# The second layer's modulation on VectorE instead of TensorE, in a kernel of two blocks

## What is computed

```python
c_act, cc_act = silu(c), silu(c_ctx)            # two vectors of 2048
for i in range(2):                              # layer 0 retention, layer 1 attention
    mod_l = c_act @ ada_w[i] + ada_b[i]         # ada_w[i] is 2048 x 6144
    mod_c = cc_act @ ada_w[i] + ada_b[i]
    sh, sc, gt = split(mod, 3)                  # shift, scale, gate, for each of the two
    h = rms_norm(x, gain[i]) * (1 + sc) + sh
    x = x + gt * mixer(h)
x = second_block(x)
```

## Time and profile before

| | |
|---|---|
| median of 3 runs | 3269.02 us |
| profiled execution, span from first to last instruction | 3265.3 us |
| TensorE busy, matmuls | 3195.3 us, 98% |
| VectorE busy | 1757.6 us, 54% |
| ScalarE busy | 1298.9 us, 40% |
| mean granted clock of TensorE | 0.995 |
| chain that ended last | TensorE 90%, VectorE 4%, ScalarE 2%, DMA 2% |
| loads of the stream | 936 chunks of 512 KB, median 4.2 us to landing |

### The profile page before, as it was taken

One profiled execution on the slowest core, in us unless ns is written; L12 is line 12 of the kernel. 1 busy time (PEld: TensorE's weight loads), 2 busy tenths in 40 slices (PEclk: granted clock), 3 DMA queues, 4 the chain that ended last, 5 costly groups with the idle time before them and its releaser, 6 DMA issues.

```text
span 3265.3 us, 48483 instructions
## 1 busy us (share of the span) xinstructions
PE 3195.3 (98%) x20556; PEld 2772.3 (85%) x20556; DVE 1757.6 (54%) x2600; ACT 1298.9 (40%) x1878; POOL 0.2 (0%) x4
## 2 busy tenths in 40 slices
PE   8999999999999999999998999999999999999998
PEld 6677777878778787777876889988999999999998
DVE  5543544444444444444446667778676665555555
ACT  4443222232322323222234645556554444444443
POOL 0000000000000000000000000000000000000000
PEclk9999999999999999999999999999999999999999
DMA  9854433233333333323334434445655545556564
GB/s 369 317 192 174 174 110 133 93 110 136 116 123 104 116 110 128 130 104 119 107 123 162 133 106 146 152 130 172 199 167 180 172 154 168 181 189 199 194 194 149
DMA packets 153928, 508.98 MB, mean 156 GB/s; under 512 B 15345, under 2 KB 35953, under 8 KB 152945
## 3 DMA queue, kind: packets, MB, share of 16 engines
q1 hardware_dynamic: 149328, 493.03, 44.4%
q10 hardware_dynamic: 4384, 12.85, 1.0%
HBM read 501.62 MB, written 4.19 MB: 155 GB/s over the span
## 4 chain that ended last, share of the span: by engine, by line
PE 90%; DVE 4%; ACT 2%; DMA 2%; issue 1%; SPq 1%; ACTq 0%; DVEq 0%
PE bank L590 28%; PE bank L592 27%; PE bank L591 27%; PE bank L652 3%; PE bank L835 1%; DMA raw<-stream 1%; DVE w_lo L1677 1%; PE bank L816 1%; ACT w_hi L1084 1%; PE bank L826 1%; SPq L563 0%; PE bank L668 0%; ACT a_s L1392 0%; DVE a_s L2084 0%; DMA raw_h<-stream 0%
## 5 line engine op out<-in xcount | busy, mean ns | idle before, releaser
L590 PE MATMUL bank<-h_hi,w_hi 128*128 128x256 f32 (+1 forms) x4032 | 1259.7, 312 | 10.7 <-DVE w_lo L1677 5.1
L592 PE MATMUL bank<-h_hi,w_lo 128*128 128x256 f32 (+1 forms) x4032 | 1239.8, 307 | 0.0
L591 PE MATMUL bank<-h_lo,w_hi 128*128 128x256 f32 (+1 forms) x4032 | 1239.1, 307 | 0.0
L1677 DVE TENSOR_TENSOR w_lo<-raw,w_hi 128x1024 fp32r<-128x1024 f32 x729 | 881.5, 1222 | 585.7 <-ACT w_hi L1084 581.3
L1084 ACT ACTIVATE w_hi<-raw 128x1024 fp32r<-128x1024 f32 x729 | 761.5, 1057 | 914.3 <-PE bank L592 568.7
L590 PEld LDWEIGHTS bank<-h_hi,w_hi 128*128 128x128 f32 x4032 | 759.3, 188 | 83.4 <-issue 39.2
L591 PEld LDWEIGHTS bank<-h_lo,w_hi 128*128 128x128 f32 x4032 | 759.6, 188 | 44.9 <-issue 3.1
L592 PEld LDWEIGHTS bank<-h_hi,w_lo 128*128 128x128 f32 x4032 | 759.1, 188 | 43.8
L590 PE MATMUL bank<-w_hi,h_hi 128*128 128x512 f32 x704 | 286.6, 407 | 12.5 <-DVE w_lo L1677 6.2
L592 PE MATMUL bank<-w_hi,h_lo 128*128 128x512 f32 x704 | 276.6, 393 | 0.0
L591 PE MATMUL bank<-w_lo,h_hi 128*128 128x512 f32 x704 | 275.9, 392 | 0.0
(11 more groups left out here) (257 smaller groups left out, 2890.4 us busy)
## 6 DMA issues: line engine op xcount, KB each, us to landing
raw<-stream SPq DMA_DIRECT2D x904, 512.0 KB, 4.2
raw_h<-stream SPq DMA_DIRECT2D x32, 512.0 KB, 10.0
res<-tokens_in ACTq DMA_DIRECT2D x4, 1024.0 KB, 8.8
vg<-mem_in ACTq DMA_DIRECT2D x4, 512.0 KB, 8.7
h_hi<-mem_kv ACTq DMA_DIRECT2D x2, 1024.0 KB, 9.7
out<-res SPq DMA_DIRECT2D x4, 512.0 KB, 3.0
mem_kv<-qk ACTq DMA_DIRECT2D x1, 1024.0 KB, 7.9
mem_kv<-vg ACTq DMA_DIRECT2D x1, 1024.0 KB, 7.5
```

The lines of the kernel that those rows point to most:

```text
L590: pe.matmul(out, sh, mh, start=start, stop=False, **checks)
L591: pe.matmul(out, sh, ml, start=False, stop=False, **checks)
L592: return pe.matmul(out, sl, mh, start=False, stop=stop, **checks)
L1677: dve.tensor_tensor(in_quarters(m.low(raw)[:, :]), m.raw[SLOT[raw]], in_quarters(m.w_hi[slot][:, :]).bitcast(F32), ALU.subtract).then_inc( ...
```

## The change

The 96 chunks of layer 1 are laid out by output feature instead of by input feature: partition p holds, for two feature tiles k = 2t and 2t+1, the weights of feature p of the tile from 512 of the 2048 inputs (a quarter q). There are 4 quarters of 24 pairs, so still 96 chunks. VectorE multiplies such a chunk with the conditioning vector, which lies as a row on every partition (`c_rows`, 128 x 1024, 512 KB, one for each quarter), and sums along the free axis, starting from the sum of the quarter before or from the bias. That is four instructions of 512 elements for a chunk. The vector is written to DRAM once at the start, and broadcast to all partitions four times from SyncE's queue. The product with the gain follows once, in the last head. TensorE's modulation matmuls and turns for layer 1, ScalarE's copies and VectorE's additions are gone.

The chunks lie behind other places: in heads 1 to 6 behind q/k tiles 0 to 3, g tiles 0 and 2, value chunks 4 to 7, and ret_out chunks 0, 2, 4, 6 and 7 (15 in a head), and in head 7 behind tiles 0 to 5. The queue of loads now waits for the last of a chunk's four instructions on VectorE ahead of loading into its slot.

```diff
-for _h in range(1, RET_HEADS - 1):
-    BESIDE[_h] = modulation_beside(places_of_head((1,) * 8, (1,) * 8), [(1, n) for n in range(3 * _h - 3, 3 * _h)])
-
-BESIDE[RET_HEADS - 1] = modulation_beside(
-    places_of_head((1,) * 6 + (0,), ()) + [(("o",), 2), (("t", 7), 0)] + [(("r", n), 2) for n in range(KT // 2)],
-    [(1, n) for n in range(18, 24)])
+for _h in range(1, RET_HEADS):
+    BESIDE[_h] = {}
+
+MOD_QUARTERS, MOD_PAIRS = 4, MOD_TILES // 2
+MOD_K = P // MOD_QUARTERS
+
+
+def modulation_on_vector():
+
+    steps = [(q, t) for q in range(MOD_QUARTERS) for t in range(MOD_PAIRS)]
+    out = {}
+    for h in range(1, RET_HEADS):
+        places = [("t", i) for i in ((0, 1, 2, 3, 4, 6) if h < RET_HEADS - 1 else range(6))]
+        if h < RET_HEADS - 1:
+            places += [("v", c) for c in range(4, 8)] + [("r", n) for n in range(0, 8, 2)] + [("r", 7)]
+        for place in places:
+            if steps:
+                out[(h, *place)] = steps.pop(0)
...
 NEEDS = []
 for _c in range(CHUNKS):
-    _n = BEFORE[_c] + 1 if BEFORE[_c] is not None and RAW_USE[BEFORE[_c]] else 0
+    _n = BEFORE[_c] + 1 if BEFORE[_c] is not None and (RAW_USE[BEFORE[_c]] or MOD_USE[BEFORE[_c]]) else 0
     NEEDS.append(max(_n, NEEDS[-1] if NEEDS else 0))
...
+RELOAD = {WHERE["ada", 0, MOD_TILES // 2 - 1][3] + 12: 0}
+for _q in range(1, MOD_QUARTERS):
+    RELOAD[FIRST["mod", _q - 1, MOD_PAIRS - 1] + SLOTS] = _q
...
         slot, before = SLOT[c], BEFORE[c]
-        if before is not None and RAW_USE[before]:
-            sp.wait_ge(s.mm, before + 1)
+        if before is not None and MOD_USE[before]:
+            sp.wait_ge(*s["modded"].at(*STREAM[before][0][1:]))
+        elif before is not None and RAW_USE[before]:
+            sp.wait_ge(s.mm, DONE[before])
         elif before is not None:
             sp.wait_ge(s.lo, Q[before] + 1)
         sp.dma_start(m.raw[slot], in_quarters(d["stream"][c])).then_inc(s.raw[slot], 16)
+        if c in RELOAD:
+            q = RELOAD[c]
+            if q == 0:
+                sp.wait_ge(s.load["c_out"], 16)
+                sp.wait_ge(*s["ada_turned"].at(*GROUPS[-1]))
+            else:
+                sp.wait_ge(*s["modded"].at(q - 1, MOD_PAIRS - 1))
+            rows = d["c_rows"][MOD_K * q:MOD_K * (q + 1), :].rearrange("a b -> (a b)").unsqueeze(0)
+            sp.dma_start(m.c_rows[:, :, :, :].rearrange("p a b c -> p (a b c)"), rows.broadcast_to([P, MOD_K * 2 * KT])
+                         ).then_inc(s.load["c_rows"], 16)
...
+            if half and n == 3:
+                act.wait_ge(*s["cond_rows"].at())
+                act.dma_start(d["c_rows"], flat(m.cond_rows)).then_inc(s.load["c_out"], 16)
...
+    def modulate(q, t):
+
+        c = FIRST["mod", q, t]
+        dve.wait_ge(s.raw[SLOT[c]], 16 * USE[c])
+        if t == 0:
+            dve.wait_ge(s.load["c_rows"], 16 * (q + 1))
+        if q:
+            dve.wait_ge(*s["modded"].at(q - 1, t))
+        for j in range(2):
+            k = 2 * t + j
+            w = m.raw[SLOT[c]][:, 2 * j:2 * j + 2, :].rearrange("p a (b c) -> p (a b) c", c=KT)
+            for b in range(2):
+                x = m.mod[1][:, k, b:b + 1]
+                start = x if q else m.bias1[:, 1, k - KT:k - KT + 1] if KT <= k < 2 * KT else m.param("ada_b1", k, 1)
+                i = dve.tensor_tensor_reduce(out=w if b else m.products[:, j, :, :], in0=w, in1=m.c_rows[:, :, b, :], scale=1.0, scalar=start,
+                                             op0=ALU.mult, op1=ALU.add, accum_out=x)
+        i.then_inc(*s["modded"].up(q, t))
+
+    def modulated():
+
+        dve.wait_ge(*s["modded"].at(MOD_QUARTERS - 1, MOD_PAIRS - 1))
+        dve.tensor_tensor(m.mod[1][:, KT:2 * KT, :], m.mod[1][:, KT:2 * KT, :],
+                          m.param("gain1").unsqueeze(2).broadcast_to([P, KT, 2]), ALU.mult).then_inc(*s["mod1_set"].up())
+
     def beside(h, *place):
         for layer, n in BESIDE[h].get(place, ((), (), ()))[2]:
             ada_add(layer, n)
+        if (h, *place) in MODS:
+            modulate(*MODS[(h, *place)])
...
             if last and n < 7:
                 for j in range(2):
                     add_square("x1", 2 * n + j, BOTH)
-                beside(h, "r", n)
+            beside(h, "r", n)
+            if last and n == 0:
+                modulated()
...
+    for c, (what, name, layer, k0, nk, n0, nn) in enumerate(STREAM):
+        if what[0] == "mod":
+            block = w[name][layer][:, n0:n0 + 2 * P].reshape(KT, P, 2, P)[:, k0:k0 + MOD_K]
+            stream[c].reshape(P, 2, MOD_K, KT)[...] = block.transpose(3, 2, 1, 0)
+            continue
```

More of the change, by code:

```diff
@@ L126 @@
 BESIDE[0] = modulation_beside(places_of_head((2, 2, 3, 2, 3, 2, 3, 3), (2, 2, 2, 2, 2, 2, 0, 0)), [(0, n) for n in range(16, 24)])
-for _h in range(1, RET_HEADS - 1):
-    BESIDE[_h] = modulation_beside(places_of_head((1,) * 8, (1,) * 8), [(1, n) for n in range(3 * _h - 3, 3 * _h)])
-BESIDE[RET_HEADS - 1] = modulation_beside(
-    places_of_head((1,) * 6 + (0,), ()) + [(("o",), 2), (("t", 7), 0)] + [(("r", n), 2) for n in range(KT // 2)],
-    [(1, n) for n in range(18, 24)])
+for _h in range(1, RET_HEADS):
[12 more added lines that the diff above has]
+                out[(h, *place)] = steps.pop(0)
+    assert not steps, len(steps)
+    return out
+MODS = modulation_on_vector()
 AV_AK = [("av", n) for n in range(5)] + [("ak", 0), ("ak", 1), ("av", 5), ("ak", 2), ("av", 6), ("ak", 3), ("av", 7)]
@@ L161, in beside @@
             ada(layer, n, (c,))
+        if (h, *slot) in MODS:
+            q, t = MODS[(h, *slot)]
+            out.append((("mod", q, t), "ada_w", 1, MOD_K * q, 0, 2 * P * t, 0))
     beside("start", "begin")
@@ L257 @@
 RAW_USE = [b[0][0] == "ada" for b in STREAM]
-SPLIT = [c for c in range(CHUNKS) if not RAW_USE[c]]
+MOD_USE = [b[0][0] == "mod" for b in STREAM]
+SPLIT = [c for c in range(CHUNKS) if not RAW_USE[c] and not MOD_USE[c]]
 Q = [0]
-for _raw in RAW_USE:
-    Q.append(Q[-1] + (not _raw))
+for _c in range(CHUNKS):
+    Q.append(Q[-1] + (not RAW_USE[_c] and not MOD_USE[_c]))
+DONE = [_c + 1 - sum(MOD_USE[:_c + 1]) for _c in range(CHUNKS)]
 WIDEST = WHERE["mv", 1][7] // (2 * WIDE) * (2 * WIDE)
@@ L358 @@
     "n_meaned", "n_rstd", "n_scaled", "merged", "m_hi", "m_lo", "final")
-LOADS = ("par", "tab", "tok0", "tok1", "tok2", "tok3", "mem_in0", "mem_in1", "mem_in2", "mem_in3", "rope0", "attn_tables", "block_tables", "kv_out", "kv_in", "out")
+LOADS = ("par", "tab", "tok0", "tok1", "tok2", "tok3", "mem_in0", "mem_in1", "mem_in2", "mem_in3", "rope0", "attn_tables", "block_tables", "kv_out", "kv_in", "c_out", "c_rows", "out")
 class Signals:
@@ L422, in __init__ @@
         modulated = nc.sbuf_base
+        self.c_rows = nc.alloc_sbuf_tensor_at("c_rows", [P, MOD_K, 2, KT], F32, offset=modulated)
         self.cond = sb("cond", [P, KT, 32])
@@ L860, in tensor_program @@
         mm.then_inc(s.mm, 1)
-        if c == 1:
-            beside(RET_HEADS - 1, "end")
     for h in range(GROUP):
@@ L1090, in done @@
     def done(what, n=2):
-        act.wait_ge(s.mm, WHERE[what][n - 1] + 1)
+        act.wait_ge(s.mm, DONE[WHERE[what][n - 1]])
     def psum(*what):
@@ L1683, in done @@
     def done(what, n=2):
-        dve.wait_ge(s.mm, WHERE[what][n - 1] + 1)
+        dve.wait_ge(s.mm, DONE[WHERE[what][n - 1]])
     def psum(*what):
@@ L1968, in vector_program @@
             weights_to(WHERE["ret_out", h][n], 1 if last and n == 7 else SLOTS)
-            dve.wait_ge(s.mm, WHERE["ret_out", h][n] + 1)
+            dve.wait_ge(s.mm, DONE[WHERE["ret_out", h][n]])
             if h == 0:
@@ L2353 @@
     stream = np.empty((CHUNKS, P, CHUNK), np.float32)
-    for c, (_, name, layer, k0, nk, n0, nn) in enumerate(STREAM):
+    for c, (what, name, layer, k0, nk, n0, nn) in enumerate(STREAM):
[3 more added lines that the diff above has]
+            continue
         block = w[name][layer][k0 * P:(k0 + nk) * P, n0:n0 + nn]
@@ L2384, in program @@
         d["out"] = nc.dram_tensor("out", (P, KT, L), F32, kind="ExternalOutput").ap()
+        d["c_rows"] = nc.dram_tensor("cond_rows", (P, 2 * KT), F32, kind="Internal").ap()
         d["mem_kv"] = nc.dram_tensor("mem_kv", (P, KT, L), F32, kind="Internal").ap()
```

22 lines of the change are left out of this document (12 added, 10 removed).

## The result

The changed kernel takes 3380.64 us (median of four runs, 3377.05 to 3385.81) against 3269.44 for the kernel before in the same session: ratio 1.0342, 95% interval 1.0328 to 1.0355, so 3.4% slower. The forecast was 3395 with a range of 3345 to 3475.

A forecast was written before the change was run, and what follows sets the result against it. TensorE was taken to bound heads 1 to 7, with VectorE's round becoming the period after the change. Terms -82 + 196.2 + 8.3 + 3.9 = +126 on 3265.3 gave 3391.7, so 3395 as median; range 3345 to 3475.

The forecast's parts named there:

- The step M: VectorE's four multiply-and-sum instructions on one modulation chunk: 4 x 0.75 = 3.0 us, bounds 2.7 to 3.7.
- The half-rate rival: Two float32 SBUF sources run VectorE's step at half rate, M 5.3 us: 3584 us, chance 8%.
- the 2% case with M at 1.4: VectorE's step takes half the cycles, so the time stays the same: 3265 us, chance 2%.
- the 3% case in which the release is hidden everywhere: Late freeing of raw slots costs nothing and all 82 us of TensorE's relief are won: 3187 us, chance 3%.
- The reload: From raw slot free through DMA and w_hi to both w_lo: 7.16 us, with a scatter of 0.2 us.
- The round: VectorE's loop in a q/k tile: 2.81 + M + 7.16 + 0.1 = 13.07 us, where TensorE takes 11.68 today.
- The head: One of heads 1 to 6: 198.3 us less TensorE's relief plus 32.7 us idle gives 220.4 us.
- The load of c_rows: Reloading the conditioning row on SyncE's queue: 1.3 us each, three times in the chain, 3.9 us.
- the rival in which only the q/k rounds bind: Loads beside v and ret_out come earlier than counted, so only q/k tiles lose time: 3257 us, chance 6%.
- 200 us of idle time: Sign to look for: TensorE idle, released by w_lo, in pieces of 2 to 5 us, some 200 in all.
- the clock costs next to nothing inside the chain: Slower TensorE costs nothing inside the chain; only at g tile 1 up to 1.7 us per head, 0 to 12.
- The theory of the release: Raw slots freed only after VectorE's step, behind eviction, swap and rotation, make VectorE's round the period in heads 1 to 7.

The follow-up runs named there:

- spread2: Changed kernel with each step ahead of VectorE's wait for TensorE and places spread more evenly, some moved to head 0 and the last head: 3182.54 us.
- warm: Changed kernel with 8 to 16 extra unread matmuls on TensorE in nine waits of heads 1 to 6 and five of head 7: 3384.91 us.
- before_late: Kernel before, extra unneeded VectorE work (2.65 us) at each place of heads 1 to 6, and slot loads waiting for that work: 3319.73 us.
- before_extra: Kernel before, with the same extra unneeded VectorE work at each place of heads 1 to 6, but no added wait: 3269.51 us.
- dup_ahead: Changed kernel with two extra 1024-element products on VectorE ahead of each of the 96 steps, before the slot is freed: 3596.5 us.
- dup_behind: Changed kernel with the same two extra products behind each of the 96 steps, after the slot is freed: 3417.38 us.
- late_spread: Changed kernel with its order kept (step behind eviction and additions) but places spread over eight tiles, value chunks and ret_out: 3285.38 us.
- spread: Changed kernel with places spread and each step ahead of VectorE's wait for TensorE: 3200.41 us.

## Why the prediction was right, step by step

**The step M.** Assumed 3.0 us, measured 2.77 (1088.83 to 1091.60): four instructions 0.67 apart and the last one's 0.75. The lower bound of 2.7 was near; the forecast was 0.23 too long. The rows by shape, 500 to 1785:

```profile
L1765 DVE CUSTOM_DVE_ANT_1 raw<-raw,c_rows,mod 128x512 f32<-128x512 f32 x138 | 103.5, 750 | 0.0
L1765 DVE CUSTOM_DVE_ANT_1 products<-raw,c_rows,mod 128x512 bf16<-128x512 f32 x138 | 103.2, 747 | 0.0
L1765 DVE DVE_READ_ACCUMULATOR2_ANT mod<- 128x1 f32 x352 | 29.9, 85 | 0.0
```

L1917, the row that I took it from, has 743 ns. The sum's read-out takes 85 ns, and the next instruction starts at the same moment (1089.50), so it costs nothing. The Trainium skill (VectorE: DVE Perf Modes, Two Vector instructions with no wait between them) says that an operation which also writes its accumulator is two instructions; the rows agree, with 85 ns for the second.

**The half-rate rival** (8%, 3584 us) falls with the same rows: 512 elements from two float32 sources take 750 ns, not 1.22 us. By the rule of the Trainium skill (Vector Engine (DVE) Microarchitecture Reference, Points that are easy to get wrong) they would have; for this operation the measurement decides against it. The page names the form S2S2D2_STT, and the trace shows this operation as CUSTOM_DVE_ANT_1; no run says whether the rule was meant for it. With M at 2.77 the 2% case with M at 1.4 falls too, and with rounds of 12.3 to 12.9 the 3% case in which the release is hidden everywhere.

**The reload.** Assumed 7.16 from the slot's release to the end of both w_lo, measured 6.8 to 7.4, 7.39 in the round shown (1091.60 to 1098.99), mean 7.0 without the round that holds a load of c_rows. To the start of the first w_hi it is 3.1 to 3.8, where the forecast had 3.5.

**The round.** Forecast 10.07 + M = 13.07. Of the 21 q/k rounds of heads 1 to 7, 20 are 12.3 to 12.9, mean 12.5. With 2.81 to the step, M 2.77 and a reload of 7.0 that is 12.6, less 0.1 by which the eviction starts ahead of w_lo's end. Of the 0.57 that I was over, 0.23 is M, some 0.16 the reload, 0.1 the semaphore, for which I had no row and which the reload as measured holds already, and the rest the overlap of eviction and w_lo.

**The relief of TensorE.** 12 chunks at 0.80 and 3 turns at 0.35 taken from 198.3 gives 187.7 for a head; `spread2` has 187.64.

**The head.** Forecast 220.4; the six are 217.8 to 222.2, mean 219.4. That the two lie so close is in part luck, since two errors of opposite sign meet in a head. From the step behind v chunk 4 to that behind the next head's last q/k tile the forecast had 145.6 us (2.4 to 148.0), and the six stretches took 139.8 to 143.1, mean 141.0, with the loads of c_rows in them: the rounds are shorter. Against that the first step comes later than forecast in every head: 5.73 us behind TensorE's start on v chunk 3 and not 2.4, so 3.3 late. The forecast left out what VectorE does there: it normalizes the head's outputs behind v chunk 2 (L2002, L2005, 980.09 to 984.99 in head 3), and only then come the w_lo of v6 and the step.

```profile
980.30 0.39 PE L631 MATMUL bank<-w_hi,h_hi 128*128 128x512 f32 x1
...
983.10 1.89 DVE L2005 TENSOR_TENSOR o_lo<-vg,o_hi 128x512 fp32r<-128x512 f32 x3
984.90 1.22 DVE L1718 TENSOR_TENSOR w_lo<-raw,w_hi 128x1024 fp32r<-128x1024 f32 x1
986.04 0.75 DVE L1765 CUSTOM_DVE_ANT_1 products<-raw,c_rows,mod 128x512 bf16<-128x512 f32 x1
```

The sum for all heads can be followed by the first tiles. First tile to first tile, head 1 to head 7, and the last head's four tiles (line L1943 and, of the kernel before, L1874; durations in ns, first and last start):

```profile
L1943 DVE TENSOR_SCALAR qk<-bank x25: 682/684/692, 431.8 to 1748.3; 128x512 f32<-128x512 f32 x25
...
L1943 DVE TENSOR_SCALAR qk<-bank x4: 683/684/685, 1748.3 to 1785.7; 128x512 f32<-128x512 f32 x4
```

```profile
L1874 DVE TENSOR_SCALAR qk<-bank x4: 691/692/692, 1623.8 to 1658.8; 128x512 f32<-128x512 f32 x4
```

The six heads take 1316.5 us and took 1190.0 (6 x 198.3): +126.5. The last head's tiles take 37.4, not 35.0: +2.4. Behind them 1590.0 us remain of 3375.7 where it was 1606.5 of 3265.3: -16.5, which fits the chunks that TensorE no longer multiplies there. Head 1's first tile comes 2.0 earlier. Together +110.4, the difference of the two spans. The forecast had +126; by its own steps the six heads were 6 x 22.1 and 3.9, so 136.5, which is 10 more than measured. What is left of it, -10, was measured as -16. So the forecast lies 16 us above the difference of the spans.

**The load of c_rows** was under-counted: 1.3 us each. In the round of head 4 that holds one, the two w_hi stand 3.26 us apart (1120.83 and 1124.09) instead of 1.27, and the round is 14.91 instead of 12.5. So 2.0 to 2.4. Three of them are 2 to 3 us more than forecast in all.

**Where the wait shows.** The places were right: TensorE's gaps in the changed kernel divide about evenly between the tiles and ret_out, which speaks against the rival in which only the q/k rounds bind (6%, 3257 us). TensorE's groups by shape, 500 to 1785, with the idle time ahead of each in the last column: the tiles, then ret_out.

```profile
L631 PE MATMUL bank<-h_hi,w_hi 128*128 128x512 f32 x732 | 295.8, 404 | 65.6 <-DVE w_lo L1718 65.6
...
L631 PE MATMUL bank<-o_hi,w_hi 128*128 128x512 f32 x384 | 163.8, 427 | 61.4 <-DVE w_lo L1718 61.3
```

The amount was not: 200 us of idle time were forecast and 127 are there. In head 4 TensorE needs 187.6 and has 222.16: 34.5 us to lose, near the forecast of 32.7. It is idle only 21.4 of them; the other 13 are a slower TensorE (clock 0.94). That the clock costs next to nothing inside the chain was argued in the forecast and fits `warm`. Behind the chain it costs what the forecast allowed: from g tile 1 to v chunk 3, where TensorE binds, four of the six heads take 62.6 us at full clock and two take 64.2, with the clock at 0.83 over the first 10 us; the forecast had up to 1.7 for each. The time lost was forecast rightly; as a sign to look for, "some 200 us of waiting" was wrong, since idle time and slow matmuls share one gap.

**The theory of the release** is shown by `before_late` against `before_extra` (the same work, one wait more, 50 us) and, in the changed kernel itself, by `dup_ahead` against `dup_behind`. That VectorE's load as such is the main cost is excluded by `before_extra` (nothing) and by `spread2`, where the same 96 steps go with the fastest time; where VectorE has no idle time, load does cost something, as the 37 us of `dup_behind` show.

What stays open: how the 95 us of the places divide between the four value tiles in a row and ret_out's steps 6 and 7, since no run moved one of them alone; and why `late_spread` stayed 15 us and `spread` and `spread2` 5 us below what the chain of rounds gave, which I can't trace to one term.

## What to carry to other kernels

When work moves from one engine to another, ask first who now frees the buffer and whether that engine also stands behind the buffer's refill: a loop through VectorE, the queue, DMA, ScalarE and VectorE again has a length of its own, and busy shares of 59% and 38% don't show it. Put the step that frees a buffer ahead of the wait for the slower engine, not behind what follows it, and let no two such steps follow each other more closely than the loop is long. The same 96 steps cost 3.4% in one order and at one set of places, and win 2.6% in another order at other places.

## What the hardware showed that was not expected

A multiply of two float32 sources in SBUF with a running sum takes 750 ns for 512 elements, as long as the operation of L1917 without a sum, which reads one source from PSUM (743 ns), and its read-out of 85 ns lies fully beside the next instruction; ScalarE's read-out had 186 ns. A broadcast load of 512 KB (c_rows, 5.0 us from issue to landing at the median against 4.2 for a chunk of the stream) delays the chunk behind it by 2.0 us, where a chunk of the stream delays the next by 1.27. And TensorE at half speed behind a gap (clock 0.94 in head 4) was all but free here: with 0.99 over the stage in place of 0.96 the time was the same to 0.2%.
